# Constant multiplies on TensorE in 18 of its waits, in a three-block transformer kernel

## The reference

```python
def hybrid_layer(x, c_act, ...):
    mod = c_act @ ada_w + ada_b                      # shift, scale, gate
    h = rmsnorm(x, norm_w) * (1.0 + scale) + shift
    u = h @ w_in                                     # all projections of the layer
    ...
    o_a = gated_delta_rule(q_a, k_a, v_a, g, beta)   # 16 heads of 128
    ...
    o_b = swa_with_sinks(q_b, k_b, v_b, sinks)       # sliding-window attention
    y = sigmoid(g_a) * (o_a @ proj_a) + sigmoid(g_b) * (o_b @ proj_b)
    return x + gate * (y @ w_out)
...
def second_block(x, p, ...):
    u = rms_norm(h, g_mix_pre) @ w_in
    attn = neighborhood_attention(...); rec = rglru_bidirectional(...) * gelu(yg)
    mixed = concatenate([rms_norm(attn, ..), rms_norm(rec, ..)]) @ w_out
    h = h + rms_norm(mixed, g_mix_post)
    ff = (silu(fn @ w_ffn_gate) * (fn @ w_ffn_up)) @ w_ffn_down     # fn = rms_norm(h)
    h = h + rms_norm(ff, g_ffn_post)
    gate = sigmoid(rms_norm(h, g_ple_pre) @ w_ple_gate)
    return h + rms_norm(gate * (p @ w_ple_proj), g_ple_post)
```

## Time and profile before

| | |
|---|---|
| median of 3 runs | 4338.17 us (4334.38 to 4339.1) |
| the profiled execution | 4339.37 us, span of its instructions 4337.6 us |
| TensorE busy | 4009.1 us, 92% of the span |
| VectorE, ScalarE, GpSimd busy | 64%, 44%, 6% |
| mean granted TensorE clock | 0.970 |

### The profile page before, as it was taken

One profiled execution on the slowest core, in us unless ns is written; L12 is line 12 of the kernel. 1 busy time (PEld: TensorE's weight loads), 2 busy tenths in 40 slices (PEclk: granted clock), 3 DMA queues, 4 the chain that ended last, 5 costly groups with the idle time before them and its releaser, 6 DMA issues.

```text
span 4337.6 us, 77491 instructions
## 1 busy us (share of the span) xinstructions
PE 4009.1 (92%) x30516; PEld 3820.7 (88%) x30516; DVE 2755.0 (64%) x3689; ACT 1910.9 (44%) x2772; POOL 266.6 (6%) x252
## 2 busy tenths in 40 slices
PE   2899999999999989999999999998888899999988
PEld 1899999998889988999999888998887788888878
DVE  7567777665668756777756566565456656565665
ACT  1444444334443344353533444354455444444464
POOL 0012121000000001212100000000000000000000
PEclk8899999999999999999999999999999999999989
DMA  9333333663349833333357433553443354545443
GB/s 391 143 126 118 130 121 121 227 252 139 130 156 329 301 122 122 125 125 122 131 195 272 156 116 136 185 178 136 157 140 121 136 183 169 180 171 186 174 144 117
DMA packets 114134, 724.41 MB, mean 167 GB/s; under 512 B 12608, under 2 KB 13056, under 8 KB 36224
## 3 DMA queue, kind: packets, MB, share of 16 engines
q1 hardware_dynamic: 88416, 639.17, 40.9%
q10 hardware_dynamic: 25504, 82.13, 5.3%
HBM read 719.09 MB, written 2.16 MB: 166 GB/s over the span
## 4 chain that ended last, share of the span: by engine, by line
PE 73%; DVE 10%; ACT 8%; issue 6%; DMA 1%; DVEq 1%; ACTq 0%; SPq 0%
PE bank L271 14%; PE bank L272 13%; PE bank L273 13%; PE bank L288 8%; PE bank L289 4%; ACT Wh L331 3%; DVE Wl L337 2%; PE bank L946 2%; PE bank L950 2%; PE bank L925 2%; DMA raw<-in_ada 1%; PE bank L2088 1%; PE bank L314 1%; PE bank L2090 1%; PE bank L2089 1%
## 5 line engine op out<-in xcount | busy, mean ns | idle before, releaser
L331 ACT CAST Wh<-raw 128x1024 fp32r<-128x1024 f32 x1140 | 1189.2, 1047 | 2093.2 <-PE bank L273 1559.6
L337 DVE TENSOR_TENSOR Wl<-raw,Wh 128x1024 fp32r<-128x1024 f32 x1140 | 1413.3, 1244 | 1002.9 <-ACT Wh L331 998.0
L271 PE MATMUL bank<-H,Wh 128*128 128x256 f32 x5536 | 1625.9, 294 | 0.5 <-ACT WS L1959 0.4
L272 PE MATMUL bank<-H,Wh 128*128 128x256 f32 x5536 | 1572.0, 284 | 0.0
L273 PE MATMUL bank<-H,Wl 128*128 128x256 f32 x5536 | 1570.8, 284 | 0.0
L271 PEld LDWEIGHTS bank<-H,Wh 128*128 128x128 f32 x5536 | 1067.8, 193 | 20.4 <-issue 19.3
L272 PEld LDWEIGHTS bank<-H,Wh 128*128 128x128 f32 x5536 | 1068.4, 193 | 11.2 <-issue 10.6
L273 PEld LDWEIGHTS bank<-H,Wl 128*128 128x128 f32 x5536 | 1066.5, 193 | 0.0
L288 PE MATMUL bank<-H,Wh 128*128 128x512 f32 x1600 | 570.1, 401 | 14.8 <-DVE Wl L337 9.3
L289 PE MATMUL bank<-H,Wl 128*128 128x256 f32 x1600 | 451.6, 282 | 0.0
L288 PEld LDWEIGHTS bank<-H,Wh 128*128 128x128 f32 x1600 | 303.5, 190 | 90.5 <-issue 14.5
(11 more groups left out here) (372 smaller groups left out, 4864.1 us busy)
## 6 DMA issues: line engine op xcount, KB each, us to landing
raw<-in_stream SPq DMA_DIRECT2D x572, 1024.0 KB, 4.8
WS<-in_ada ACTq DMA_DIRECT2D x94, 512.0 KB, 6.5
raw<-in_ada SPq DMA_DIRECT2D x32, 1024.0 KB, 7.5
gm_more<-in_ada ACTq DMA_DIRECT2D x20, 512.0 KB, 7.1
WS<-rows_d ACTq DMA_DIRECT2D x16, 512.0 KB, 4.8
KR<-in_ada ACTq DMA_DIRECT2D x14, 512.0 KB, 6.4
X<-in_x_t SPq DMA_DIRECT2D x1, 2048.0 KB, 17.4
WS<-in_rpb ACTq DMA_DIRECT2D x8, 256.0 KB, 2.9
```

The costliest lines, as they stand in the source:

```text
L271: pe.matmul(out[:, 0:T], wh, xh[:, kt, :], start=first, stop=False)
L272: pe.matmul(out[:, 0:T], wh, xl[:, kt, :], start=False, stop=False)
L331: act.copy(Wh[:, n % 4, :], raw[:, (sbk + 2) % 4, k * (D // 2):(k + 1) * (D // 2)]).then_inc(hi_ready, 1)
L337: dve.tensor_tensor(Wl[:, n % 4, :], raw[:, (sbk + 2) % 4, k * (D // 2):(k + 1) * (D // 2)], Wh[:, n % 4, :].bitcast(F32), ALU.subtract).t ...
```

## The change

A helper `pe_spin` multiplies `ones` by 256 columns of the constants, `count` times, into bank `B[5]`; nothing waits for the result and nobody reads it. It is called at 18 places of TensorE's program with a count written at each. One of them lies in a loop of two rounds, so it runs 19 times; the counts sum to 181 multiplies.

```diff
+        def pe_spin(pe, count):
+
+            for _ in range(count):
+                pe.matmul(B[5][:, 0:T], ones, C[:, 0:T], start=True, stop=True)
@@ pe_pre, end
                     S.done(i, "pe", "v_tok")
+            pe_spin(pe, 17)
             S.wait(pe, "dve", "last_less", l)
@@ pe_gdn
                 if n == SCAN + 4:
+                    if not chain:
+                        pe_spin(pe, 11)
                     F.wait(pe, "act", "sq", f)
@@ pe_out, end
             if l == 0:
+                pe_spin(pe, 3)
                 pe_stat(pe, l + 1, Q_OUT - 1, out_sq[(Q_OUT - 1) % 2])
+                pe_spin(pe, 7)
                 return
             S = st_fin
             S.start("pe")
+            pe_spin(pe, 6)
             S.wait(pe, "dve", "acc14")
@@ pe_na
                     if h and n == 3:
+                        if h == 4:
+                            pe_spin(pe, 7)
                         S.wait(pe, "dve", f"prob{h - 1}", i)
@@ pe_second
         def pe_second(pe):
+            pe_spin(pe, 12)
             with pe.Fori(0, 2) as i:
                 pe_na(pe, i)
...
             pe_mix(pe)
+            pe_spin(pe, 6)
             pe_total(pe, st_p[0])
+            pe_spin(pe, 13)
             pe_sums(pe, st_n[2])
+            pe_spin(pe, 8)
             feed_forward(pe, pe_gu, None, pe_dn)
+            pe_spin(pe, 6)
             pe_ff_total(pe)
+            pe_spin(pe, 13)
             pe_sums(pe, st_n[3])
+            pe_spin(pe, 8)
             pe_gate(pe)
@@ the tensor program
             pe_ada(pe, 1)
+            pe_spin(pe, 11)
             for l in range(LAYERS):
                 pe_pre(pe, l)
                 pe_gdn(pe, l, 0, True, False)
+                pe_spin(pe, 9)
                 with pe.Fori(1, PAIRS) as i:
```

## The result

The changed kernel takes 4301.24 us (median of 6 runs, 4297.7 to 4305.18); the kernel before, run beside it, 4335.82 (6 runs, 4333.62 to 4339.1). The ratio is 0.992 with a 95% interval of 0.991 to 0.993: 34.6 us or 0.8% faster. The profiled execution took 4302.99 us with a span of 4301.2. One slow execution of the kernel before (4463.11 us, mean clock 0.862) and one of the second experiment (8914.74 us) stand far outside the rest and are left out of every median.

What follows compares the result with a forecast made beforehand. TensorE and its clock bound the kernel almost everywhere. Halving 88.66 us of low clock gains 44.3; less 6.3 of limits and 3.0 of remaining falls, 35.0. From 4338.2 that gives 4303 us, range 4296 to 4315 (8 in 10).

Steps and rivals of the forecast that it cites:

- the spins' own gain: Behind TensorE's 19 waits: 88.66 us of low-clock stretches halve to 44.3, less 6.3 and 3.0, leaving 35.0 us.
- The clock is what is gained: Behind the filled waits TensorE runs at full clock from the first multiply; mean granted clock 0.970 to about 0.99.
- The price of a multiply and the rests: Each added multiply takes 0.43 us at full clock, 0.87 at half; most waits keep 0.1 to 0.8 us.
- The first spin: First layer's norm, 11 multiplies: starts at half clock, takes 7.5 us in a 6.7 us wait, 0.6 to 0.8 late.
- Where the clock may still fall: After 767's added multiplies and ahead of 2122, little work or rest lets the clock fall; 3.0 us lost.
- the two runs of 767: Delta rule's first projections: one clock fall counted across both executions, costing 1.7 us.
- The fall at 2122: After feed-forward, 2.2 us left idle lets the clock fall once; costs 1.3 us with the next spin's lateness.
- The clips: Gains capped by other work: first norm 1.2, second 0.8, totals 0.9 and 0.6, sums of squares 2.0 us.
- a sign of being wrong: Would refute the forecast: issue waits ahead of 767 or 522, 0.50 clock in spins, new DVE line 337 waits; unpriced.
- Rival 1: Delta rule, behind 767, 966 and 913: clock held but gain swallowed by DVE or other chains; 4318 us, chance 0.11.
- Rival 2: All spins: constants don't hold the clock, spins run at half clock, 67 us late; 4405 us, chance 0.05.
- Rival 3: Clock falls at 767 twice, 2122 and three 0.7 or 0.8 rests; 9 more lost, 4312 us, chance 0.08.

Runs made afterwards that it cites:

- the second experiment: Changed kernel plus 45 one-column multiplies at the start of TensorE's program, putting the feed-forward loop back at its earlier place in a packet; 4313.61 us, ratio 0.9952.

## Why the prediction was right, and where only its total was

- **The size.** Forecast 4303 with 4296 to 4315, measured 4301.24. The forecast's 35.0 us was the spins' own gain, and that is 25.3 in the traces and 23.0 by the experiment with the loop placed as before. Some 9 us came from the placement of the feed-forward loop, which the prediction did not have at all. Two errors of opposite sign made the total fit, by luck. With the loop placed as before it was 4313.61, just inside the range.
- **The clock is what is gained.** Right: 0.970 to 0.983, with the first multiplies behind the spins at full pace (46 where there were 25). The forecast 0.99 was a little high.
- **The price of a multiply and the rests.** Right to about 0.1 us: 0.70 and 0.71 measured behind 767 for 0.7 forecast, 0.35 for 0.4, 0.31 for 0.3, 0.64 for 0.6, 0.40 for 0.4, 0.85 for 0.8, a lateness of 0.17 for 0.2 at `pe_na`, 0.68 for 0.7, 2.25 for 2.2. One differs, the second one after the mixer, 0.95 for 0.1, where the sum waits for ACT's tiles. The first spin was to be at half clock at first and the projection 0.6 to 0.8 late: it starts at 109.30 instead of 108.67, 0.63 late.
- **Where the clock may still fall.** This is the step that was mis-sized most. I counted one fall in the two runs of 767 and 1.7 us for it. Both fell, the second for 6.83 us: the two places gave 2.1 and 0.4 us where my sum had 3.9 and 3.8, 7.7 less the 1.7. So 3.5 of the missing 9.7 us (35.0 less 25.3) are here. The fall at 2122 came as forecast. It is a matter of chance from one execution to the next: of the other two profiles of the changed kernel one has the same three falls and the other only the second of those behind 767.
- **The clips.** The first norm gained 1.25 (1.5 forecast) and the second 0.6 (0.9), so the low part of the next weights does bound them. After the mixer 3.2 had come of the 3.9, and then TensorE waits 2.44 us for a tile of DVE at 3409.95 where it waited 0.75 before, which leaves 1.6. The row of the timeline after:

```profile
3409.95 0.47 PE L288 MATMUL bank<-H,Wh 128*128 128x512 f32 x1 [2.44 <-DVE WS L329]
```

And the same instruction before:

```profile
3433.89 0.47 PE L288 MATMUL bank<-H,Wh 128*128 128x512 f32 x1 [0.75 <-DVE WS L324]
```

  I had named new waits for DVE behind the pairs as a sign of being wrong, for another line (337), and priced none: this one costs about 1.7 us. After feed-forward 3.5 came of 4.1, at 1616 and `pe_na` 3.5 of 4.3, at 1681 4.2 of 5.7, where 0.7 more had been gained and was given back at the next wait (line 1871). Each of these is smaller than half of its low stretch; I did not follow the other reasons one by one, and they stay open.
- **Rival 1**, the gain swallowed in the delta rule: no. 966 gave 2.5 and 2.4 where 2.6 and 2.5 were forecast, 913 gave 1.6 twice for 1.7. TensorE paces that part.
- **Rival 2**, constants don't hold the clock: no. The clock rises amid a spin and holds in it. Its price was real, though, as the one-column version shows: spins that don't hold it outlast their waits and end slower than before.
- **Rival 3**, more falls than counted: partly. It named 767 twice and 2122, and these three fell; none of the rests of 0.7 or 0.8 elsewhere did in this profile.

## What to carry to other kernels

What filler in a wait can win back is not the wait but the slow stretch behind it: lay a window from the first multiply to the moment at which the clock is full again, take half of its length, and then look for what else the faster stretch meets (here the low part of the next weights, a table load, a tile of DVE), since such things and the falls that remained made 25 us out of 44.3 here. Filler has to be tried for whether it holds the clock (256 columns did here, one column did not, though both kept the engine busy), and it must end before the wait does; count it in us at the clock that it will really have. And when an edit adds instructions ahead of a loop, compare the waits at the loop's turns in both traces before crediting the edit with the whole difference (the total of this forecast was right by such a term), and if they differ, separate the two with filler at the start of the program.

## What the runs showed of the hardware

- A turn of TensorE's loop cost 1.4 to 2.3 us of standing still in some placements and 2.8 to 3.5 in others. At each of the 12 long turns (the kernel before, the second experiment and the half spins) two instruction packets of 16.4 KB start within 0.4 us of each other, 0.6 to 1.6 us before the round's last multiply ends; at each of the 32 short ones (eight profiles of the other kernels with a loop) a single one does. The packets and the placement go together, and moving the loop by the instructions of 19, 45 or 50 multiplies switches it; how the fetch works inside no trace shows.
- The clock fell behind 10 of these 12 long turns and behind 3 of the 32 short ones, but not behind rests of 2.8 and 2.5 us in the version with half spins. What else decides, the runs don't settle; the places differ between the profiles of one kernel, and three falls in its attention make 4.5 of the 5.9 us between two of them.
- Back-to-back multiplies of one column let the clock fall though the profile shows TensorE busy without a gap (at 166.4, 5.1 us into such a run); multiplies of 256 columns with the same constants held it through 7.5 us ahead of the same wait.
